# A hybrid attention and convolution layer: another lead-in, with the modulation rows and the gate row multiplied on TensorE

## The reference

```python
shift, scale, gate = split(silu(c) @ w_ada + b_ada, 3)            # one row each, 1024 wide
h = rms_norm(x, norm_w) * (1 + scale) + shift                     # x is 1024 x 1024, float32
q, k, v, gate_a, u, gate_b = split(h @ w_in)                      # widths 512, 128, 128, 512, 1024, 512
q, k = rope(rms_norm(q)), rope(rms_norm(k))                       # per head of 64
y_a = sliding_window_attention_with_sinks(q, k, v) * silu(gate_a) # window 128, blocks of 128
a, g = split(u)                                                   # 512 channels each
z = depthwise_conv(a * sigmoid(g), 31 taps) + conv_b              # causal
y_b = silu(layer_norm(z)) * silu(gate_b)
out = x + gate * (concat(y_a, y_b) @ w_out)
```

## Time and profile before

| what | value |
|---|---|
| median of 3 runs | 521.14 us (520.79 to 522.5) |
| the profiled execution | 519.75 us, its span 518.0 us |
| TensorE busy | 432.6 us (84%), 2025 products |
| VectorE busy | 369.0 us (71%), 451 instructions |
| ScalarE busy | 192.1 us (37%) |
| GpSimd busy | 239.3 us (46%) |
| mean granted TensorE clock | 0.951 |

### The profile page before, as it was taken

How to read it: one execution, slowest core, us unless ns; L and a number is a source line. 1 busy time by engine, 2 the same in 40 slices (tenths; PEclk the granted TensorE clock), 3 DMA queues, 4 the chain that set the end, 5 groups by cost and what they waited for, 6 DMA issues and landing times.

```text
span 518.0 us, 5540 instructions
## 1 busy us (share of the span) xinstructions
PE 432.6 (84%) x2025; PEld 336.9 (65%) x2025; DVE 369.0 (71%) x451; ACT 192.1 (37%) x424; POOL 239.3 (46%) x158
## 2 busy tenths in 40 slices
PE   0368899998888198689879699999799996999996
PEld 0256787886677086656656556777467774788885
DVE  0689825499999969999999997939955259812111
ACT  4224529344010015366636757742134233410000
POOL 1441200789716354475456636771412364595121
PEclk9999989998979779699989999999899998899999
DMA  7999600445200000000400303131302040333111
GB/s 237 290 278 316 196 35 0 150 136 168 84 0 6 0 6 7 5 6 1 128 1 1 82 0 83 41 83 40 83 0 81 1 158 4 123 121 143 40 42 61
DMA packets 46375, 41.94 MB, mean 81 GB/s; under 512 B 10425, under 2 KB 41197, under 8 KB 46348
## 3 DMA queue, kind: packets, MB, share of 16 engines
q1 hardware_dynamic: 46348, 41.59, 26.7%
HBM read 37.38 MB, written 4.19 MB: 80 GB/s over the span
## 4 chain that ended last, share of the span: by engine, by line
DVE 43%; PE 28%; issue 14%; POOL 7%; ACT 4%; SPq 2%; DMA 2%; POOLq 0%; ACTq 0%; DVEq 0%
DVE cacc L1176 15%; DVE z L1176 8%; PE pm L512 6%; PE pm L514 5%; PE pm L513 5%; POOL xr L472 3%; DMA slab<-in_w_ada 2%; ACT sel L961 2%; DVE ada_acc L1107 2%; POOL h L454 2%; DVE nmx L1254 1%; POOL wts L367 1%; DVE gb L1363 1%; DVE rot L1225 1%; DVE rot L1222 1%
## 5 line engine op out<-in xcount | busy, mean ns | idle before, releaser
L367 POOL TENSOR_TENSOR wts<-raw,wts 128x1024 fp32r<-128x1024 f32 x30 | 83.5, 2797 | 104.1 <-ACT wts L829 104.1
L512 PE MATMUL pm<-h,wts 128*128 128x512 f32 x224 | 94.8, 423 | 12.6 <-POOL wts L367 4.1
L1176 DVE SCALAR_TENSOR_TENSOR cacc<-z,cw,cacc 128x1024 f32<-128x1024 f32 x60 | 98.5, 1687 | 0.2
L514 PE MATMUL pm<-h,wts 128*128 128x512 f32 x224 | 90.7, 405 | 0.0
L513 PE MATMUL pm<-h,wts 128*128 128x512 f32 x224 | 90.4, 404 | 0.0
L1176 DVE SCALAR_TENSOR_TENSOR z<-z,cw 128x1024 f32<-128x1024 f32 x60 | 80.4, 1378 | 0.1
L695 PE MATMUL pm<-wts,h 128*128 128x256 f32 (+1 forms) x128 | 48.6, 379 | 21.9 <-DVE rot L1232 20.4
L512 PEld LDWEIGHTS pm<-h,wts 128*128 128x128 f32 x224 | 44.1, 197 | 28.9 <-issue 6.6
L514 PEld LDWEIGHTS pm<-h,wts 128*128 128x128 f32 x224 | 43.9, 196 | 9.9
L513 PEld LDWEIGHTS pm<-h,wts 128*128 128x128 f32 x224 | 44.3, 198 | 9.3 <-issue 0.8
L829 ACT ACTIVATE wts<-raw 128x1024 fp32r<-128x1024 f32 x30 | 30.7, 1052 | 49.1 <-PE pm L514 26.9
(11 more groups left out here) (179 smaller groups left out, 852.1 us busy)
## 6 DMA issues: line engine op xcount, KB each, us to landing
raw<-in_w_in SPq DMA_DIRECT2D x18, 512.0 KB, 4.1
slab<-in_w_ada SPq DMA_DIRECT2D x16, 512.0 KB, 7.7
xs<-in_x SPq DMA_DIRECT2D x8, 512.0 KB, 6.8
raw<-in_w_ada SPq DMA_DIRECT2D x8, 512.0 KB, 3.8
xr<-in_x SPq DMA_DIRECT2D x8, 512.0 KB, 3.3
out<-xr SPq DMA_DIRECT2D x16, 256.0 KB, 2.0
raw<-in_w_in SPq DMA_DIRECT2D x16, 128.0 KB, 2.8
raw<-in_w_out SPq DMA_DIRECT2D x8, 256.0 KB, 3.8
```

The costliest lines, as they stand in the source:

```text
L367: gp.tensor_tensor(wts[:, slot, 1, ks, :], raw[:, raw_at["w", i] % 3, :].rearrange("p (k n) -> p k n", k=4), wts[:, slot, 0, ks, :].bitcas ...
L512: pe.matmul(out, hi_w, hi_x, start=first, stop=False)
L514: return pe.matmul(out, hi_w, lo_x, start=False, stop=last)
L1176: ins = dve.scalar_tensor_tensor(out=acc, in0=src, scalar=cw[:, i, j:j + 1], in1=acc, op0=ALU.mult, op1=ALU.add)
```

## The change

The lead-in now does six column tiles for each `k` (channels 0, 1 and 2 of the convolution, value and gate, first half). Their weights come in strips of 768 columns for one `k` (`("e", k)` in `raws`, `early_hi`, `early_lo`) instead of units of 256 columns for four `k`. The sums of the slabs leave VectorE: TensorE multiplies `cact` by the slab itself (`ada_rows`, eight products of 32 equal columns, four at a time in different column groups), ScalarE copies the rows (`ada_copy`), and TensorE turns them into columns with `quad` (`ada_cols`). The slabs are loaded as two of 1 MB and three of 2 MB. The transposes use one bank. ScalarE writes only the rounded tile, and VectorE makes the rest in two operations. Two of four x tiles have their squares summed on VectorE (`mean_squares`), which also scales and adds EPS. The gate row is formed on TensorE (`gate_rows` between the channel tiles, `gate_cols`), `gdiag` is made by ScalarE in eight copies, and `gate_product` and `gacc` are gone. The channel tiles come in another order, `LAG` is 8 and the tap steps ahead of the loop are 8, 2, 1, 4, 1, 2 instead of 6, 6, 2, 2, 2, 1, 3. The banks and the numbers of units, pieces and tiles are renumbered to match.

```diff
+        raws = [("e", k) for k in range(KT)] + [("w", 0), ("w", 1)] + [("g", i) for i in range(KT)]
+        raws += [("w", i) for i in range(2, len(pieces))]
...
-        LAG = 6
+        LAG = 8
...
+            for t in range(4):
+                load_x(t)
+            load_slab(0, 0, P, 0)
             sp.dma_start(cwrows[0:TAPS, :], conv_w[0]).then_inc(s_cw, 16)
             load_raw(0)
+            load_slab(0, P, P, 1)
+            load_slab(1, 0, 2 * P, 2)
             load_raw(1)
-            load_slab(1)
             load_raw(2)
-            load_slab(2)
+            sp.wait_ge(p_arow, 2)
+            load_slab(2, 0, 2 * P, 3)
             load_raw(3)
+            sp.wait_ge(p_arow, 3)
+            load_slab(3, 0, 2 * P, 4)
+            for t in range(4, NT):
+                load_raw(t)
+                load_x(t)
             sp.dma_start(wqk[:, 0, :], q_norm_w.to_broadcast([P, DH])).then_inc(s_bc, 16)
...
+            def early_lo(k):
+                gp.wait_ge(a_hi, k + 1)
+                gp.tensor_tensor(wts[:, 1:4, 1, k, :].rearrange("p s (a n) -> p a s n", a=2),
+                                 raw[:, raw_at["e", k] % 3, 0:2 * EARLY * P].rearrange("p (a s n) -> p a s n", a=2, s=EARLY),
+                                 wts[:, 1:4, 0, k, :].rearrange("p s (a n) -> p a s n", a=2).bitcast(F32),
+                                 ALU.subtract).then_inc(g_lo, 1)
...
-            for i in range(1, KT):
-                gp.wait_ge(a_gp, i + 1)
-                if i > 1:
-                    gp.wait_ge(g_gp, i)
-                ins = gp.tensor_tensor(gacc[:, :], gacc[:, :], raw[:, raw_at["g", i] % 3, :], ALU.add)
-                ins.then_inc(g_gp, 1 + (i == 1))
...
+            def ada_rows(j, first, n, s):
+
+                if s == 0:
+                    pe.wait_ge(d_cact, 1)
+                    pe.wait_ge(a_cols, 1)
+                else:
+                    pe.wait_ge(d_ab, (0, 2, 4, 8, 12)[s])
+                pe.wait_ge(s_slab[s], 32)
+                for t in range(KT):
+                    q = 32 * (t % 4)
+                    o = pv[q:q + 32, :].rearrange("p (a n) -> p a n", a=2)[:, :, first:first + n]
+                    last = pe.matmul(o, cact[:, t:t + 1].to_broadcast([P, 32]), slab[:, j % 2, t, :, first:first + n],
+                                     start=(t < 4), stop=(t >= 4))
+                last.then_inc(p_arow, 1)
...
             def ada_cols(k):
 
-                if k == 0:
-                    pe.wait_ge(d_cact, 1)
-                    pe.wait_ge(a_cols, 3)
-                if k >= 2:
-                    pe.wait_ge(d_ab, 2 * (k - 1))
-                pe.wait_ge(s_slab[k % 3], 32 * (k // 3 + 1))
-                pe.wait_ge(d_ada, 8 * k + 8)
+                pe.wait_ge(a_arow, k + 1 if k < 2 else k // 2 + 2)
+                if k >= 2 and k % 2:
+                    pe.wait_ge(d_ab, 2 * k)
                 for part in range(2):
-                    o = ada_bank(k)[:, part:part + 1]
-                    pe.matmul(o, slab[:, k % 3, 7, part, :], cact[:, 7:8], start=True, stop=False)
-                    last = pe.matmul(o, ada_acc[:, k % 2, 0, part * P:(part + 1) * P], ones[:, 0:1], start=False, stop=True)
+                    last = pe.matmul(pv[:, part:part + 1], rowsb[:, k // 2 % 2, part, k % 2 * P:(k % 2 + 1) * P],
+                                     quad[:, 0:1], start=True, stop=True)
                 last.then_inc(p_ada, 1)
 
...
+            def early_extra(k, e):
+
+                if e == 0:
+                    if k == 0:
+                        ada_rows(0, P, P, 1)
+                    elif k in (1, 3, 5):
+                        ada_rows((k + 1) // 2, 0, 2 * P, (k + 3) // 2)
+                    elif k < KT - 1:
+                        ada_cols(k + 1)
+                if e == 1 and k < KT - 1:
+                    x_transposes(0, k + 1)
+                if e == 2 and k in (0, 1, 3, 5):
+                    ada_cols(k + 1)
+
             for k in range(KT):
-                if k + 1 < KT:
-                    x_transposes(k + 1)
-                    ada_cols(k + 1)
                 pe.wait_ge(d_hlo, k + 1)
-                if k % 4 == 0:
-                    pe.wait_ge(g_lo, 2 if k == 0 else 4)
-                for bank, slot, col in early:
-                    last = channel_step(bank, slot, col, 0, k)
+                pe.wait_ge(g_lo, k + 1)
+                for e, (o, ct, col) in enumerate(early):
+                    if k == 0 and e == 4:
+                        pe.wait_ge(a_cw, 1)
+                    last = channel_step(o, ct, col, 0, k)
                     if k == KT - 1:
                         last.then_inc(p_main, 1)
-
...
+            def late_transposes(first):
+                def each(k):
+                    if k % 2 == 1:
+                        x_transposes(1, first + k // 2)
+                return each
+
+            def gate_rows(pair):
+
+                if pair == 0:
+                    pe.wait_ge(a_tanh, 3)
+                    pe.wait_ge(d_hlo, 2 * KT)
+                for i in range(2):
+                    r = raw_at["g", 2 * pair + i]
+                    pe.wait_ge(s_raw[r % 3], raw_due[r])
+                for i in range(2):
+                    r = raw_at["g", 2 * pair + i]
+                    for half in range(2):
+                        q = 64 * i + 32 * half
+                        last = pe.matmul(tr[q:q + 32, half, :], cact[:, 2 * pair + i:2 * pair + i + 1].to_broadcast([P, 32]),
+                                         raw[:, r % 3, half * HALF:(half + 1) * HALF], start=(pair == 0), stop=(pair == 3))
+                last.then_inc(p_grow, 1)
+
+            def gate_cols():
+
+                pe.wait_ge(a_grow, 1)
+                for i in range(KT):
+                    last = pe.matmul(tr[:, 0, i:i + 1], grow[:, i % 4 * P:(i % 4 + 1) * P], quad[:, 1 + i // 4:2 + i // 4],
+                                     start=True, stop=True)
+                last.then_inc(p_gcol, 1)
+
 
...
+            channel_tile(pv[:, :], 3, P, 0, late_transposes(0))
             pe.wait_ge(a_tanh, 1)
-            channel_tile(6, pm[:, 0, :], 1, 0, 1)
+            channel_tile(ps[:, 0, :], 3, 0, 0, late_transposes(4))
             pe.wait_ge(a_tanh, 2)
-            channel_tile(7, pm[:, 1, :], 0, 0, 1)
+            channel_tile(ps[:, 1, :], 0, P, 1)
+            gate_rows(0)
             pe.wait_ge(d_glu, 1)
-            channel_tile(8, pm[:, 2, :], 1, P, 1)
+            channel_tile(pm[:, 0, :], 0, 0, 1)
+            gate_rows(1)
             pe.wait_ge(d_glu, 2)
-            channel_tile(9, ps[:, 0, :], 0, P, 1)
+            channel_tile(pm[:, 1, :], 1, P, 1)
+            gate_rows(2)
+            pe.wait_ge(d_glu, 3)
+            channel_tile(pm[:, 2, :], 1, 0, 1)
+            gate_rows(3)
+            pe.wait_ge(a_tanh, 4)
+            channel_tile(pv[:, :], 2, P, 1)
+            gate_cols()
+            pe.wait_ge(d_glu, 4)
+            channel_tile(ps[:, 0, :], 2, 0, 1)
+            pe.wait_ge(a_tanh, 5)
+            channel_tile(ps[:, 1, :], 3, P, 1)
+            pe.wait_ge(d_glu, 5)
...
+            def early_hi(k):
+                r = raw_at["e", k]
+                act.wait_ge(s_raw[r % 3], raw_due[r])
+                act.activation(wts[:, 1:4, 0, k, :].rearrange("p s (a n) -> p a s n", a=2),
+                               raw[:, r % 3, 0:2 * EARLY * P].rearrange("p (a s n) -> p a s n", a=2, s=EARLY),
+                               ACT.Copy).then_inc(a_hi, 1)
+
+            def ada_copy(s):
+
+                act.wait_ge(p_arow, s + 1)
+                first, n = ((0, P), (P, P), (0, 2 * P), (0, 2 * P), (0, 2 * P))[s]
+                if s >= 3:
+                    act.wait_ge(p_ada, 2 * (s - 2))
+                act.activation(rowsb[:, (0, 0, 1, 0, 1)[s], :, first:first + n],
+                               pv[:, :].rearrange("p (a n) -> p a n", a=2)[:, :, first:first + n], ACT.Copy).then_inc(a_arow, 1)
+
+            def modulate(half, k):
+
+                act.wait_ge(p_xT, half * KT + k + 1)
+                act.wait_ge(d_ab, 2 * k + 2)
+                sl = slice(half * HALF, (half + 1) * HALF)
+                act.activation(h[:, 0, k, sl], tr[:, 0, :], ACT.Identity, scale=modA[:, k:k + 1],
+                               bias=modB[:, k:k + 1]).then_inc(a_h32, 1)
 
...
+            early_hi(0)
+            modulate(0, 0)
+            for k in range(KT):
+                if k in (0, 1, 3, 5):
+                    ada_copy((k + 3) // 2 if k else 1)
+                if k < KT - 1:
+                    modulate(0, k + 1)
+                    early_hi(k + 1)
+                if k in (5, 6):
+                    sum_x(2 * k - 6)
...
+            tanh_g(0, 0, ps[:, 0, :], 1)
+            tanh_g(1, 0, ps[:, 1, :], 3)
+            tanh_g(2, 0, tr[:, 1, :], 5)
+            w_hi(0)
+            w_hi(1)
+            for k in range(KT):
+                modulate(1, k)
+                if k == 5:
+                    tanh_g(3, 0, pv[:, :], 7)
```

(61 more changed lines are left out.)

365 lines of the change are left out of this document (144 added, 221 removed).

## The result

The changed kernel takes 543.91 us (median of 4 runs, 542.21 to 544.8), the kernel before 520.96 in the same job: a ratio of 1.0452, 95% interval 1.0427 to 1.0477, so 4.5% slower. The forecast was 532 with a range of 516 to 546. The direction held, but the loss is 22.9 us, where 11 to 12.5 were worked out. The profiled span grew by 24.6 us, to 542.6.

A forecast was written before the change was run, and what follows sets the result against it. VectorE's order of work was taken as the bound, with the lead-in deciding its first tap. `rope(0)` 0.5 us later, the convolution's end 10 and the restart 2 made 12.5 on 519.75: 532, range 516 to 546.

The forecast's parts named there:

- VectorE's stretch to `rope(0)`: From the first tap to the end of `rope(0)`: 61 us, taken between 58.5 and 64.5, against 83.8 before.
- the debt of the ten taps: End of the convolution: ten taps put off to n=12 and n=13 make `s23` end 10 us later.
- the restart: TensorE before `ln_mean`: after standing 15 us it restarts at the lower clock, costing 2 us.
- the stop behind the six tiles: Lead-in: TensorE stands 7 us while the next weights wait for VectorE's squares, GpSimd's power and three tanh.
- the pitch of the late transposes: Lead-in, second half: one bank makes each transpose wait for the split before, 2.72 us per period, seven periods.
- the ninth and tenth tile with the gate rows: End of the lead-in: two tiles of 5.5 us each and first gate rows of 0.95.
- the start of the first tap: End of the lead-in: VectorE's first tap at 121.5 us, 23.3 later than 98.2.
- Row tiles 1 to 6: Lead-in: three pairs of 15.3 us, 9.1 with `ada_rows` and 6.2 without, all at the higher clock.
- Rival 4: Lead-in: TensorE's idling brings the slow clock, half of the row tiles hit, +9 us, 541; chance 0.12.
- The late transposes and tiles 7 and 8: Lead-in: the two tiles run from 88.8 to 109.6 us, paced by second-half transposes through one bank.
- PE's waits in them ended by POOL's early weights: Row tiles of the lead-in: TensorE's next row tile stands behind GpSimd's `early_lo`, priced at 2.2 us.
- Rival 3: TensorE sets the lead-in, VectorE's stretch is 58.5 or less, half the debt hidden: 512, faster; chance 0.18.

The follow-up runs named there:

- run 1: Changed kernel with ScalarE copying the early weights of k+1 ahead of `ada_copy` and the modulation of k+1: 536.81 us, ratio 1.0332.
- run 2: Changed kernel with six extra TensorE products behind the last one of row tiles 0 to 6, altering one column tile's values: 538.34 us, ratio 1.0349.
- run 5: Changed kernel with the second half's transposes taking turns between two banks: 538.06 us, ratio 1.0341.
- run 6: Changed kernel with the second half's squares two row tiles earlier and weight copies `w_hi(0)`, `w_hi(1)` ahead of the three tanh: 536.58 us, ratio 1.0323.
- run 8: Changed kernel with the edits of run 1, run 5, run 6 and run 7 together: 531.64 us, ratio 1.0212.
- run 9: Changed kernel with VectorE's split as one operation from PSUM, ScalarE making shift minus high half in one more operation: 547.33 us, ratio 1.0533.
- run 10: Changed kernel with the one-operation split of run 9 and the edits of run 1, run 5 and run 6: 519.18 us, ratio 0.998.
- run 11: Kernel of run 10 with six products by zeros behind row tiles 0, 1, 3 and 5: 520.16 us, ratio 0.9992.
- run 3: Changed kernel with four more tap steps at n = 10, so four fewer left at n = 13: 542.22 us, ratio 1.0427.
- run 7: Changed kernel with VectorE's split as multiply and add from PSUM, then a two-input subtract in SBUF: 549.3 us, ratio 1.0546.
- Run 4: Kernel before with only the tap plan changed, `LAG` 8 and ten taps fewer ahead of `rope(0)`: 520.62 us against 519.79, ratio 1.0018.
- run 12: Kernel of run 10 with the layer norm's mean two projection tiles later on TensorE, squares and variance one tile later: 514.95 us, ratio 0.9892.

## Why the prediction was half right

Time minus the start of the first second-half GLU is 412.0 us in the changed kernel, and between 411.1 and 412.5 in runs 1, 2, 5, 6, 8, 9, 10 and 11 (run 3: 412.8; run 7: 415.3, but in its profiled execution the span minus the GLU is 411.3, against 410.7 for the changed kernel). The GLU moves over 27 us in these runs, and the end moves with it. So all behind the lead-in behaves as fixed work, and the lead-in's length is passed on one to one. Against the kernel before (520.96 - 98.20 = 422.8) that rest is 10.8 us shorter, which pays for a third of the 33.7 us that the lead-in grew.

**What held.** VectorE's stretch to `rope(0)` (60.7, forecast 61, its waits and its contention off in opposite directions), the debt of the ten taps (10.6, forecast 10), the restart (2.6, forecast 2). Run 4 shows the first two as a pair that cancels. Row tiles at the higher clock (9.3 and 6.3, forecast 9.1 and 6.2), the stop behind the six tiles (6.76, forecast 7), its cause, the pitch of the late transposes (2.84, forecast 2.72), and the ninth and tenth tile with the gate rows (12.3 us, forecast 11.9) held too. Eight products of `ada_rows` took 1.85 us at the higher clock, near the 1.75 from the earlier trace rows. An estimate by the ratio for three tiles in the Trainium skill (TensorE: Matmul & The Clock Gate, Measured speedup vs the span model) gives 2.2; the measurement decides.

**What failed is the start of the first tap: 121.5 forecast, 131.9 measured.** The step that failed is that the sum prices TensorE's products in the lead-in at the higher clock throughout, and charges no restart behind the 7 us stop. These terms were too small:

- *Row tiles 1 to 6*: 46 us forecast, 52.3 measured (32.81 to 85.09). The sum prices every product at the higher clock, and in k = 1, 2 and 6 TensorE's work or part of it was at the lower. Rival 4 had this mechanism, priced at 9 us with half of the products hit, and given a chance of 0.12 on the strength of one window of the kernel before at 1.00. Three of the six row tiles were hit. By their longer pitches it cost 5.3 us; run 2, which fills the waits, got 5.6 back. The other 0.9 is 9.3 and 6.3 instead of 9.1 and 6.2. The window in the earlier trace rows was a weak witness: row tiles 3, 4 and 5 here were at 1.00 too, with row tile 2 at 0.60 beside them.
- *The late transposes and tiles 7 and 8*: 20.8 forecast, 23.3 measured (96.23 to 119.57). About 1.6 of the 2.5 is TensorE's restart at the lower clock behind the 7 us stop (granted 0.52 from 96.2 to 102). The prediction charged such a restart at `ln_mean`, after a stop, and forgot it here. The rest is the pitch, 0.12 longer seven times.
- *First product and row tile 1*: 0.8 later; the first product itself came at 22.39, 1.9 later than forecast. *Row tile 7 and the stop*: 0.3 longer. *The last tiles*: 0.4 longer.

Together 10.4, the missing 10.4; some 7 of it is products at the lower clock that the sum had at the higher. In the row tiles the 2.2 us for GpSimd "with 0.3 for DVE's `tensor_scalar` in its way" was nearly the right length with the parts the other way round: it is VectorE's operation that is held, for nearly all of GpSimd's 1.80, and it ends 0.3 us behind. So the sign "PE's waits in them ended by POOL's early weights" failed: VectorE's split ended them. That is why run 9 could not be foreseen from the sum, and why the length was right all the same, which was luck.

That the pair of channel tile 0 is complete later, and that this decides, was right. Rival 3 put the point at which it decides at a first tap before about 108 us: run 10 has 107.88 and is 0.2% below the kernel before.

## What to carry to other kernels

Where no engine is full, write out the chain from engine to engine and find every branch that ends within a few tenths of it: shortening one branch can give nothing or a loss (run 9), and the same edit beside one that shortens the other branch was part of the largest gain (run 10). When work is taken from the bounding engine, ask first when that engine gets its first piece under the new order; 23 us less work on VectorE did not pay for starting 34 us later. Look for a wait of known length with independent work queued behind it on the same engine: moving that work ahead brought 4 us (run 12).
